# A two-layer diffusion trunk: modulation panels multiplied on VectorE, layer 0's last panels spread over three stages

## The chip, the core and the metric

The kernel runs on one core of a Trainium2 chip. The metric is the time of one execution on the device, in microseconds. It is given as the median of several runs; the profile is of one more execution.

## The reference

One step of a trunk with two layers over 640 tokens of width 1024: 128 prompt tokens and 512 latent tokens, in float32. In each layer a modulation vector of 6 x 1024 numbers is made from each of two conditions (one for the prompt, one for the latents), and then

```
mod = silu(cond) @ w_ada + b_ada
sh1, sc1, g1, sh2, sc2, g2 = split(mod, 6)
h = rmsnorm(x, norm_mix) * (1 + sc1) + sh1
x = x + g1 * mixer(h)
h = rmsnorm(x, norm_ffn) * (1 + sc2) + sh2
x = x + g2 * ((silu(h @ w_gate) * (h @ w_up)) @ w_down)
```

Layer 0's mixer is one input projection, then attention (8 heads of 64, the prompt over itself, the latents over the latents and 128 cached tokens) beside a state space scan in both directions (8 heads, chunks of 128 tokens, two groups of B and C), and one output projection. For each chunk the scan makes exp of differences of running sums of the decays, times C.B, times x, and adds C times the decayed state. Layer 1's mixer is retention with 4 heads. The FFN is 2816 wide.

## The kernel before, in words

Every engine has its instructions written out by hand, in one order per engine, with semaphores between them. The activations lie feature-major in SBUF; x is `xT`, the modulated h is split in a high and a low part (`h_hi`, `h_lo`), and so is every panel of weights: SyncE loads 1 MB (1024 x 256) into `raw0` or `raw1`, ScalarE writes `w_hi` (`split_hi`, L1086), VectorE `w_lo` (`split_lo`, L1448), and TensorE multiplies three products (`tile_a`, L579, 48 matmuls of 320 columns for 128 features; `tile_b`, L605, for 128 tokens in the input projection). VectorE subtracts a panel's low part only after ScalarE's high part, and that one is written when TensorE has left the slot's older panel.

**Modulation.** `w_ada` of a layer is 24 panels of 256 columns. `ada_job` (L638) multiplies one on TensorE: `scond`, the SiLU of both conditions in 2 of 32 columns, is the stationary operand, and eight fp32 matmuls of 256 columns go to four strips of partitions of one bank, `ROWS`. ScalarE copies the rows (`ada_rows`, L1091), and before the next panel `ada_turn` (L613) turns them to columns by two fp32 matmuls that also add the four strips. The columns collect in `ADA`. Layer 0's panels 0 to 7 are multiplied at the start (they give the first shift and scale). Its panels 8 to 23 are multiplied in the scan, from three buffers (`ada_raw0`, `raw0`, `raw1`), one or two per unit. Layer 1's panels 0 and 1 are multiplied in layer 0's output projection, 2 to 23 in layer 0's FFN, one behind each gate/up panel, from two buffers.

**The stages.** Times are those of the profile. Up to 63 us setup, first panels, norm. To 156 the input projection: three panels of q, k, v token by token (`tile_b`, five tiles each), then x, B, C, z. To 189 the convolution, the normed and rotated q and k, and dt, mostly on VectorE. To 286 the attention: 20 pairs, four of the prompt and 16 of the latents. In pair p TensorE makes the scores (`scores_of`, L739), VectorE the maximum, ScalarE the exponentials with their sum, GpSimd a diagonal of 1/sum; then TensorE turns the probabilities of pair p-1 (`turn_of`, L769) and multiplies pair p-2 by v (`att_of`, L758).

The scan runs from 286 to 375. TensorE makes running sums (L791), turned x and B, and C.B (L811). VectorE spreads the running sums per head (`by_head`, L1728) and makes xw (`weighted`, L1738); GpSimd makes xd, ten instructions (L2082), as soon as x is there. `ecum_of` (L830) and ScalarE give the decays on the states' partitions, `local_states` (L839) a chunk's own states into three banks, `step` (L1749, L1754) runs the states through the chunks. Then ten units of five chunks and two groups: `exponents` (L869 to L871, three matmuls for each direction: the sums per head, minus the sums along the tokens, the mask), ScalarE's exponential (L1285), VectorE's product with C.B (L1799, `m_ready`), and `outputs` (L893, L897). `exponents` of the next unit stand before a unit's panel and its `outputs`. VectorE also multiplies the decays by C (L1781) and reads y (`y_in`, L1787).

To 447 the output projection in two halves with the norm of y between them, `into_x` (L1542) and squares on VectorE. Then rms, `modulate` (L1508, L1520) and layer 0's FFN to 960: three chunks of 8, 8 and 6 gate/up panels, each chunk followed by four down panels. In an iteration ScalarE takes SiLU of the first tile, VectorE multiplies with the second (`gu32`, L1856), subtracts the low part of the next weight panel and of gu (L1865). Layer 1 follows, up to 2098; its panels are not touched.

SyncE's queue issues all loads in one order. A load waits for its buffer, and what is behind it in the queue waits too: `panel` for `w_lo` of the slot, `ada_panel` for the panel two before.

## Time and profile before

| | |
|---|---|
| median of 3 runs | 2093.09 us (2089.72 to 2094.92) |
| the profiled execution | 2099.29 us, its span 2097.7 us |
| granted TensorE clock, mean | 0.967 of full |
| busy, share of the span | TensorE 95%, VectorE 49%, ScalarE 27%, GpSimd 3% |
| the chain that ended last | TensorE 89%, VectorE 6%, ScalarE 2% |

Times in the profile are from the span's start. PE is TensorE's products, PEld its weight loads, DVE VectorE, ACT ScalarE, POOL GpSimd, SPq SyncE's queue. An fp32 matmul of 4 bytes without the r format shows as two records: an `ada_turn` has four, a panel's eight matmuls sixteen. Matmuls overlap, so the time of one is read from start to start.

### The profile page before, as it was taken

What the parts mean: (1) busy time and instruction counts of PE and PEld (TensorE: products, weight loads), DVE (VectorE), ACT (ScalarE), POOL (GpSimd) and SP (SyncE); (2) the same over time, 40 slices, a digit from 0 to 9 for tenths busy, and PEclk for the clock granted to TensorE, in tenths of its full rate; (3) what the DMA queues carried; (4) which work ended last, traced back from release to release, by engine and by line L of the source; (5) the groups of instructions that cost most, each with busy time, mean ns of one, the idle gap of its engine ahead of it and who ended that gap; (6) DMA issues with size and microseconds to landing.
All of it is one profiled execution on the core that took longest, in us unless ns stands there. A gap on an engine that the chain in (4) does not pass through costs nothing.

```text
span 2097.7 us, 32318 instructions
## 1 busy us (share of the span) xinstructions
PE 1989.3 (95%) x13455; PEld 1850.9 (88%) x13455; DVE 1032.8 (49%) x1472; ACT 563.3 (27%) x736; POOL 71.3 (3%) x118
## 2 busy tenths in 40 slices
PE   6999989889999999997999999999998999999997
PEld 3897856889999999997889889889888999999997
DVE  5377564782243234246646546645657235225335
ACT  2325432222212221223322332332333221221221
POOL 0001230000000000001010010010000000000000
PEclk7898988989999999999999999999998999999998
DMA  8320007344433433423212222122111222222211
GB/s 262 89 83 21 2 23 239 86 141 121 155 106 100 121 101 101 144 77 110 81 66 70 76 69 82 61 69 82 61 53 48 80 80 61 80 80 71 71 60 51
DMA packets 213535, 185.29 MB, mean 88 GB/s; under 512 B 10865, under 2 KB 198705, under 8 KB 213425
## 3 DMA queue, kind: packets, MB, share of 16 engines
q1 hardware_dynamic: 209504, 172.27, 26.7%
q0 software_dynamic: 3616, 11.29, 1.6%
q8 instruction: 89, 1.46, 0.3%
q14 instruction: 21, 0.17, 0.0%
q10 hardware_dynamic: 305, 0.10, 0.0%
HBM read 176.42 MB, written 7.21 MB: 88 GB/s over the span
## 4 chain that ended last, share of the span: by engine, by line
PE 89%; DVE 6%; ACT 2%; issue 1%; DMA 1%; SPq 0%; POOL 0%; ACTq 0%; DVEq 0%; POOLq 0%
PE acc L579 63%; PE acc L982 4%; PE mix L638 2%; PE acc L1013 2%; PE acc L1029 2%; PE acc L605 2%; PE acc L592 2%; PE acc L769 2%; PE mix L1002 1%; PE mix L982 1%; PE mix L739 1%; PE acc L758 1%; PE mix L613 1%; PE mix L653 1%; DVE h_lo L1520 1%
## 5 line engine op out<-in xcount | busy, mean ns | idle before, releaser
L579 PE MATMUL acc<-h_hi,w_hi 128*128 128x320 f32 x2144 | 495.6, 312 | 22.2 <-DVE h_lo L1520 6.3
L579 PE MATMUL acc<-h_lo,w_hi 128*128 128x320 f32 x2144 | 491.1, 310 | 4.3 <-issue 4.3
L579 PE MATMUL acc<-h_hi,w_lo 128*128 128x320 f32 x2144 | 490.2, 310 | 0.0
L579 PEld LDWEIGHTS acc<-h_hi,w_hi 128*128 128x128 f32 x2144 | 358.3, 189 | 37.3 <-issue 29.1
L1086 ACT ACTIVATE w_hi<-raw 128x2048 fp32r<-128x2048 f32 x112 | 214.3, 1914 | 653.0 <-PE acc L579 634.4
L579 PEld LDWEIGHTS acc<-h_hi,w_lo 128*128 128x128 f32 x2144 | 360.4, 189 | 4.7 <-issue 4.7
L579 PEld LDWEIGHTS acc<-h_lo,w_hi 128*128 128x128 f32 x2144 | 360.5, 189 | 0.0
L1448 DVE TENSOR_TENSOR w_lo<-raw,w_hi 128x2048 fp32r<-128x2048 f32 x112 | 256.7, 2292 | 199.4 <-ACT w_hi L1086 195.7
L1856 DVE TENSOR_TENSOR gu<-silu_g,acc 128x640 f32<-128x640 f32 x44 | 36.1, 821 | 416.8 <-PE acc L579 408.3
L1542 DVE SCALAR_TENSOR_TENSOR xT<-acc,mod,xT 128x128 f32<-128x128 f32 (+2 forms) x288 | 108.8, 433 | 140.6 <-PE acc L579 139.0
L579 PE MATMUL acc<-gu_hi,w_hi 128*128 128x320 f32 x704 | 160.7, 309 | 0.7 <-DVE gu_lo L1865 0.7
L579 PE MATMUL acc<-gu_hi,w_lo 128*128 128x320 f32 x704 | 160.4, 309 | 0.0
L579 PE MATMUL acc<-gu_lo,w_hi 128*128 128x320 f32 x704 | 160.2, 309 | 0.0
L579 PEld LDWEIGHTS acc<-gu_hi,w_hi 128*128 128x128 f32 x704 | 117.5, 188 | 2.2 <-issue 1.2
L579 PEld LDWEIGHTS acc<-gu_lo,w_hi 128*128 128x128 f32 x704 | 117.7, 188 | 0.0
L579 PEld LDWEIGHTS acc<-gu_hi,w_lo 128*128 128x128 f32 x704 | 117.6, 188 | 0.0
L1322 ACT ACTIVATE silu_g<-acc 128x640 f32<-128x640 f32 x44 | 31.1, 706 | 212.2 <-PE acc L579 205.9
L1470 DVE TENSOR_TENSOR sq_sum<-sq_sum,sq 128x640 f32<-128x640 f32 x99 | 81.7, 825 | 3.4
L1468 DVE TENSOR_TENSOR sq<-xT 128x640 f32<-128x640 f32 x84 | 69.4, 826 | 11.8 <-DVE xT L1542 6.6
L579 PE MATMUL acc<-yg_hi,w_hi 128*128 128x320 f32 x256 | 58.6, 311 | 3.3 <-DVE yg_lo L2015 3.3
L579 PE MATMUL acc<-yg_hi,w_lo 128*128 128x320 f32 x256 | 58.2, 309 | 0.0
L579 PE MATMUL acc<-yg_lo,w_hi 128*128 128x320 f32 x256 | 58.1, 309 | 0.0
(322 smaller groups left out, 2449.6 us busy)
## 6 DMA issues: line engine op xcount, KB each, us to landing
ada_raw<-in_l_w_ada_dram SPq DMA_DIRECT2D x64, 512.0 KB, 4.6
raw<-in_l_w_in_dram SPq DMA_DIRECT2D x64, 512.0 KB, 4.4
raw<-in_l_w_gate_dram SPq DMA_DIRECT2D x44, 512.0 KB, 4.0
raw<-in_l_w_up_dram SPq DMA_DIRECT2D x44, 512.0 KB, 5.3
raw<-in_l_w_down_dram SPq DMA_DIRECT2D x32, 512.0 KB, 4.5
raw<-in_l_w_out_dram SPq DMA_DIRECT2D x24, 512.0 KB, 4.5
raw<-in_l_w_ada_dram SPq DMA_DIRECT2D x22, 512.0 KB, 4.7
raw<-in_l_w_down_dram SPq DMA_DIRECT2D x16, 384.0 KB, 3.7
```

What stands on the lines that cost most here:

```text
L579: last = mm(acc[:, 2 * r + b, 0:HALF], w[:, k * cols + col:k * cols + col + P], x[:, k, b * HALF:(b + 1) * HALF], start=(k == 0 and n == 0 ...
L592: last = mm(acc[:, 2 * r[c] + b, 0:HALF], w[:, k * W + c * P:k * W + (c + 1) * P], x[:, k, b * HALF:(b + 1) * HALF], start=(k == 0 and n = ...
L605: last = mm(acc[:, 2 * r, 0:W], x[:, k, tok(t)], w[:, k * W:(k + 1) * W], start=(k == 0 and n == 0), stop=(k == KT - 1 and n == 2))
L638: last = mm(ROWS[32 * q:32 * q + 32, :], scond[:, k, :], w[:, k * W:(k + 1) * W], start=(turn == 0), stop=(turn == KT // 4 - 1))
L769: last = mm(acc[:, g, m * P:(m + 1) * P], probs[:, p % 2, g, m * P:(m + 1) * P], rdiag[:, (2 * p + g) % 4, :], start=True, stop=True)
L982: last = mm(V_BANKS[t], a[:, x, tok(t)], w[:, cols], start=(x == 0 and n == 0), stop=(x == KT - 1 and n == 2))
L1013: last = mm(acc[:, v, :], a, x, start=(b == 0 and k == 0 and m == 0), stop=(b == 1 and k == 1 and m == 2))
L1086: act(w_hi[s][:, :], raw[s][:, :], ACT.Copy).then_inc(S[f"w_hi{s}"], ac.up(f"w_hi{s}"))
L1448: ins = tt(w_lo[s][:, :], raw[s][:, :], w_hi[s][:, :].bitcast(f32), ALU.subtract)
L1468: tt(sq[:, :], src, src, ALU.mult).then_inc(S["dve"], v.up("dve"))
L1470: tt(sq_sum[:, :], sq_sum[:, :], sq[:, :], ALU.add).then_inc(S["dve"], v.up("dve"))
L1542: ins = st3(xT[:, d, dst], acc[:, 2 * r + b, src], mod[l][:, GA[m] + d, c:c + 1], xT[:, d, dst], ALU.mult, ALU.add)
```

## The change

- Layer 1's 24 panels are multiplied on VectorE in layer 0's FFN. `ada_products`: for each of 8 blocks of 128 rows and each condition, one instruction over 128 x 256 multiplies the panel's block by the condition's column (a scalar per partition) and adds it to `ada_sum` (in `tbuf`). `ada_add` on TensorE then sums over the partitions: four fp32 matmuls with `ada_sum` stationary and one column of ones, straight to `ADA`. One panel stands ahead of each gate/up iteration on VectorE, its add behind that iteration's tiles on TensorE; two panels stand in the first and the second down projection. The two jobs in the output projection, the row copies on ScalarE and SyncE's two loads ahead of the FFN are gone.
- Layer 0's panels 8 to 11 are multiplied in the same way in the input projection: products before the first, behind the first (one) and behind the second panel's low part (two), adds behind tiles (1,1), (1,4), (2,2), (2,4).
- Panels 12 to 14 stay TensorE jobs, in the attention's pairs 1 to 3 of the prompt. Panels 15 to 23 stay in the scan: three by the first exponents, then one per unit up to unit 6.
- The scan is reordered. An exponent is two matmuls: `L_all` and `R_all` hold on 128 partitions what the first two of three held on 64; ScalarE fills their constant halves during the attention and four scaled copies in the scan. Decays and exponents go through one ring of four banks. `local_states` uses one bank and waits for the step before. The prompt's units come between the steps. GpSimd's xd waits until four xw are made.

```diff
+            for n in ADA_DVE[0:2]:
+                ada_panel(w_ada, n * W)
...
+                if j == 3:
+                    for n in ADA_DVE[2:]:
+                        ada_panel(w_ada, n * W)
...
+            for n in ADA_PE:
+                k = ring_slot(n)
+                if n >= ADA_PE[3]:
...
+                else:
+                    eng.wait_ge(S["ada_used"], ADA_PE[0] - 1)
...
-            for n in range(2):
-                ada_panel(I["l1_w_ada"], n * W)
...
-                                ada_panel(I["l1_w_ada"], (i * 2 + s + f0 + 2) * W)
+                                ada_panel(I["l1_w_ada"], (i * 2 + s + f0 + m) * W)
...
+                        if l == 0 and m < 2 and j == 0:
+                            ada_panel(I["l1_w_ada"], (f0 + nf + m) * W)
...
+            def ada_add(l, n, b_):
+
+                eng.wait_ge(S["row_in"], pe.next("row_in"))
+                for b in range(2):
+                    for c in range(2):
+                        last = mm(ADA[:, l, bass.ds(n * 2 + b, 1), c:c + 1].rearrange("p o c -> p (o c)"),
+                                  ada_sum[b_][:, c, b * P:(b + 1) * P], ones[:, 0:1], start=True, stop=True)
+                last.then_inc(S["ada_turned"], pe.up("ada_turned"))
...
+            pe.skip("ada_in0", 32 * 2)
+            ADA_PLACES = [(1, 1), (1, 4), (2, 2), (2, 4)]
             for j in range(8):
...
                         tile_b(s, t, "h_ready" if j == 0 and t == 0 else None)
+                        if (j, t) in ADA_PLACES:
+                            n = ADA_DVE[0] + ADA_PLACES.index((j, t))
+                            ada_add(0, n, n % 2)
...
+            jobs = iter(ADA_PE)
+            ada_next = lambda: (lambda n: ada_job(0, n, n > ADA_PE[0]))(next(jobs))
             for p in range(NP + 2):
+                if p == 4:
+                    ada_turn(0, ADA_PE[2])
                 if p < NP:
                     scores_of(p)
+                if 1 <= p < 4:
+                    ada_next()
...
+            def ring(k):
+
+                kind, t, g = RING[k]
+                out = acc[:, k % 4, :]
+                if k >= 4:
+                    eng.wait_ge(S["arg_read"], k - 3)
+                if kind == "ecum":
+                    eng.wait_ge(S["r_ready"], R_ORDER.index(t) + 1)
+                    ins = mm(out, sel_wide[:, g, :], R_of(t), start=True, stop=True)
+                else:
+                    (t, g), d = chunks[t], g
+                    eng.wait_ge(S["r_ready"], R_ORDER.index(t) + 1)
+                    mm(out, L_all[:, 2 * d + g, tok(t)], R_of(t), start=True, stop=False)
+                    ins = mm(out, ident_r[:, :], mask_r[:, d, :].unsqueeze(1).broadcast_to([P, 4, P]), start=False, stop=True)
+                ins.then_inc(S["arg_made"], pe.up("arg_made"))
...
+                if s > 1:
+                    eng.wait_ge(S["z_ready"], s - 1)
...
-                    out, dg = acc[:, (2 * u + d) % 4, :], 2 * d + g
-                    mm(out, sel_dg[0:64, dg:dg + 1].broadcast_to([64, P]), R_of(t), start=True, stop=False)
-                    mm(out, cumx[:, tok(t)], sel_of[0:64, dg, :].unsqueeze(2).broadcast_to([64, 4, P]), start=False, stop=False)
-                    ins = mm(out, ident_r[:, :], mask_r[:, d, :].unsqueeze(1).broadcast_to([P, 4, P]), start=False, stop=True)
-                    ins.then_inc(S["arg_made"], pe.up("arg_made"))
...
-                        eng.wait_ge(S["s_out_ready"], 1)
+                        eng.wait_ge(S["g_read"], 4)
...
+            eng.wait_ge(S["xt_read"], TT)
+            c_dot_b(0, [acc[:, 2 + g, 0:P] for g in range(2)]).then_inc(S["g_made"], pe.up("g_made"))
+            eng.wait_ge(S["fill_ready"], 1)
+            ring(0)
+            ring(1)
+            ada_next()
+            eng.wait_ge(S["g_read"], 4)
+            ring(2)
+            ring(3)
+            eng.wait_ge(S["l_ready"], 1)
+            ring(4)
+            ring(5)
+            local_states(1)
+            for k in range(6, 10):
+                ring(k)
+            ada_next()
+            ring(10)
+            ring(11)
+            outputs(0)
+            local_states(2)
+            ada_next()
+            for k in range(12, 14):
+                ring(k)
+            outputs(1)
+            local_states(3)
+            local_states(4)
+            for u in range(2, 2 * TT):
                 if u + 1 < 2 * TT:
-                    exponents(u + 1)
-                ada_next()
+                    for d in range(2):
+                        ring(ring_at["expo", u + 1, d])
+                if u < 7:
+                    ada_next()
                 outputs(u)
-                if ADA_AFTER[u] > 1:
-                    ada_next()
             ada_turn(0, ADA_JOBS - 1)
...
-                if j == 0:
-                    eng.wait_ge(S["mod_read"], pe.next("mod_read"))
-                ada_job(1, j, j > 0)
...
                     if l == 0:
-                        ada_job(1, f + s_ + 2, slot=s_)
...
+                        ada_add(1, f + s_ + m, (s_ + m) % 2)
...
+                        if l == 0 and m < 2 and j == 1:
+                            ada_add(1, f0 + nf + m, m % 2)
...
+                if 1 <= p < 4:
+                    ada_rows()
...
+                if 6 <= p < 10:
+                    act(L_all[0:64, p - 6, :], sel_dg[0:64, p - 6:p - 5].broadcast_to([64, N]), ACT.Copy)
+                if 10 <= p < 15:
+                    ins = act(four(R_all[64:128, p - 10, :]), sel4[64:128, :].unsqueeze(2).broadcast_to([64, 4, P]), ACT.Copy)
+                    if p == 14:
+                        ins.then_inc(S["fill_ready"], ac.up("fill_ready"))
...
+            exponentials(0)
+            exponentials(1)
+            ada_rows()
+            eng.wait_ge(S["cumT_lo"], ac.next("cumT_lo"))
+            for dg in range(4):
+                ins = act(L_all[64:128, dg, :], cumx[64:128, :].bitcast(f32), ACT.Copy, scale=sel_dg[64:128, dg:dg + 1])
+            ins.then_inc(S["l_ready"], ac.up("l_ready"))
+            for k in range(2, 10):
+                exponentials(k)
+            ada_rows()
+            exponentials(10)
+            exponentials(11)
             ada_rows()
             for s in range(2):
...
+            eng.wait_ge(S["ce_ready"], 8)
...
+            ada_slot = [0]
+
+            def ada_products():
+
+                s = ada_slot[0] % 2
+                ada_slot[0] += 1
+                eng.wait_ge(S[f"ada_in{s}"], v.next(f"ada_in{s}", 32))
+                eng.wait_ge(S["ada_turned"], v.now("ada_turned", 1))
+                for k in range(KT):
+                    if k:
+                        eng.wait_ge(S[v.last], v.ended())
+                    for c in range(2):
+                        w = ada_raw[s][:, k * W:(k + 1) * W]
+                        if k == 0:
+                            ins = ts(ada_sum[s][:, c, :], w, scond[:, k, c:c + 1], None, ALU.mult)
+                        else:
+                            ins = st3(ada_sum[s][:, c, :], w, scond[:, k, c:c + 1], ada_sum[s][:, c, :], ALU.mult, ALU.add)
+                    ins.then_inc(S["dve"], v.up("dve"))
+                eng.wait_ge(S[v.last], v.ended())
+                eng.sem_inc(S["ada_used"], v.told("ada_used"))
+                eng.sem_inc(S["row_in"], v.told("row_in"))
+                v.skip("ada_turned")
...
+            ada_products()
...
+                for _ in range((1, 2, 0, 0, 0, 0, 0, 0)[j]):
+                    ada_products()
...
+            for t in R_ORDER[0:2]:
+                by_head(t)
             eng.wait_ge(S["wst_exp"], v.next("wst_exp"))
...
             weighted(1)
-            by_head(2)
-            by_head(3)
+            for t in R_ORDER[2:]:
+                by_head(t)
             weighted(2)
-            by_head(4)
             eng.wait_ge(S["s0_ready"], v.next("s0_ready"))
             step(1)
+            eng.wait_ge(S["g_read"], 4)
+            decayed_gram(0)
             weighted(3)
             weighted(4)
             step(2)
+            decayed_gram(1)
             step(3)
             eng.wait_ge(S["loc_made"], 4)
-            ins = eng.tensor_copy(s_out[:, :, :].rearrange("p h d -> p (h d)"), LOCAL[4])
...
-            eng.wait_ge(S["g_read"], 4)
             eng.wait_ge(S["c2_ready"], 1)
+            decayed_c(1, 0)
+            decayed_c(1, 1)
             for u, (t, g) in enumerate(chunks):
-                for d in range(2):
-                    eng.wait_ge(S["e_ready"], 2 * u + d + 1)
-                    ins = tt(e_of(u, d), e_of(u, d), G[:, g, t, :].unsqueeze(1).broadcast_to([P, 4, P]), ALU.mult)
-                    ins.then_inc(S["m_ready"], v.up("m_ready"))
+                if t == 0:
+                    continue
+                decayed_gram(u)
...
+                    if l == 0:
+                        per |= {"dve": 2 + 2 * KT, "ada_in0": 32, "ada_in1": 32, "ada_turned": 2, "row_in": 2, "ada_used": 2}
...
+                            if l == 0:
+                                ada_products()
...
+                        if l == 0 and m < 2 and j == 0:
+                            ada_products()
...
+            eng.wait_ge(S["xw_ready"], 4)
```

## Rows read from the trace of the kernel before

**Rows 1.** TensorE's timeline in layer 0's FFN: start us, us, engine, line, operation, out<-in, count.
```profile
506.36 0.50 PE L613 MATMUL mix<-fold,ada_row 128*128 128x2 f32 x4
506.79 1.07 PE L638 MATMUL mix<-ada_raw,scond 128*32 128x256 f32 x16
...
521.97 0.50 PE L613 MATMUL mix<-fold,ada_row 128*128 128x2 f32 x4
```

**Rows 2.** The chain that ended last, in order of time: layer 1's FFN.
```profile
1621.61 408.55 PE acc L579 x2784
```

**Rows 3.** Stretches of the scan: us, busy PE PEld DVE ACT POOL, clock, DMA share, GB/s.
```profile
286.00:325.00 39.00, 31.36 (x181) 17.61 (x183) 27.19 (x33) 12.65 (x26) 13.80 (x10) 0.71 0.17 55
325.00:379.00 54.00, 50.81 (x537) 33.13 (x534) 28.34 (x52) 18.82 (x38) 0.00 (x0) 0.97 0.84 254
```

**Rows 4.** The timeline of the scan's first half; in brackets idle time before, and its releaser.
```profile
292.68 1.29 DVE L1738 TENSOR_TENSOR xw<-x_tok,wdt 128x512 f32<-128x512 f32 x2
...
294.28 13.80 POOL L2082 TENSOR_TENSOR xd<-x_tok,dt_tok 128x512 f32<-128x512 f32 x10 [12.98 <-ACT x_tok L1251]
...
304.73 4.50 DVE L1738 TENSOR_TENSOR xw<-x_tok,wdt 128x512 f32<-128x512 f32 x4
307.32 1.98 PE L839 MATMUL mix<-xw,b_tok 128*64 128x256 f32 x8 [5.25 <-DVE xw L1738]
```

**Rows 5.** VectorE's groups by form: count, busy us, mean ns, idle before.
```profile
L1640 DVE SCALAR_TENSOR_TENSOR conv<-xpad,vec,conv 128x644 f32<-128x644 f32 x24 | 20.3, 886 | 0.4
...
L1520 DVE SCALAR_TENSOR_TENSOR h_lo<-tbuf,mod,h_hi 128x512 fp32r<-128x512 f32 x16 | 11.9, 746 | 0.0
...
L1520 DVE SCALAR_TENSOR_TENSOR h_lo<-tbuf,mod,h_hi 128x128 fp32r<-128x128 f32 x16 | 5.6, 347 | 1.1 <-ACT h_hi L1115 1.1
...
L1636 DVE TENSOR_SCALAR conv<-xpad,vec 128x644 f32<-128x644 f32 x6 | 3.0, 551 | 0.0
```

**Rows 6.** VectorE's timeline at the start of layer 0's FFN and inside it.
```profile
470.39 1.01 DVE L1520 SCALAR_TENSOR_TENSOR h_lo<-sq,mod,h_hi 128x128 fp32r<-128x128 f32 x2 [0.23 <-ACT h_hi L1115]
...
475.43 0.82 DVE L1856 TENSOR_TENSOR gu<-silu_g,acc 128x640 f32<-128x640 f32 x1 [4.02 <-PE acc L592]
...
526.33 0.82 DVE L1865 TENSOR_TENSOR gu_lo<-gu,gu_hi 128x640 f32 x1
```

**Rows 7.** ScalarE's timeline in the out projection.
```profile
432.66 1.92 ACT L1086 ACTIVATE w_hi<-raw 128x2048 fp32r<-128x2048 f32 x1 [12.66 <-DMA raw<-in_l_w_up_dram]
```

**Rows 8.** ScalarE's and VectorE's timeline in the input projection.
```profile
91.28 0.38 ACT L1158 ACTIVATE qkv<-acc 128x256 f32<-128x256 f32 x1 [2.50 <-PE acc L605]
...
93.73 2.29 DVE L1448 TENSOR_TENSOR w_lo<-raw,w_hi 128x2048 fp32r<-128x2048 f32 x1 [12.11 <-ACT w_hi L1086]
```

**Rows 9.** Busy time by stretch in the prompt's attention; one row of ScalarE's timeline in a later pair.
```profile
190.00:192.00 2.00, 0.57 (x5) 0.38 (x5) 0.76 (x5) 1.29 (x5) 0.74 (x2) 1.00 0.00 0
...
194.00:196.00 2.00, 2.00 (x10) 1.51 (x8) 0.52 (x3) 1.07 (x5) 1.82 (x7) 0.50 0.00 0
...
246.84 0.80 ACT L1227 ACTIVATE probs<-mix,nmax 128x640 f32<-128x640 f32 x1 [2.80 <-DVE nmax L1700]
```

**Rows 10.** TensorE's timeline in the scan's second half: third output, a unit, the last output.
```profile
336.09 0.66 PE L893 MATMUL mix<-tbuf,xd 128*64 128x128 f32 x8
...
345.58 0.49 PE L869 MATMUL acc<-R_lat,sel_dg 64*128 64x512 f32 x1
...
347.63 0.50 PE L613 MATMUL mix<-fold,ada_row 128*128 128x2 f32 x4
...
349.06 0.66 PE L893 MATMUL mix<-tbuf,xd 128*64 128x128 f32 x8
...
350.52 0.49 PE L869 MATMUL acc<-R_lat,sel_dg 64*128 64x512 f32 x1
...
374.80 0.39 PE L897 MATMUL mix<-ecum,ada_raw 128*64 128x128 f32 x4
```

**Rows 11.** Busy time by stretch just before the scan's clock rises.
```profile
324.00:326.00 2.00, 2.00 (x20) 1.33 (x14) 0.29 (x1) 1.19 (x3) 0.00 (x0) 0.50 0.07 11
```

More of the change, by code:

```diff
@@ L140 @@
     "vec_T vec_read cond no_cond": "small vectors turned, copied; SiLU of the conditions; the zeros beside them",
-    "ada_used row_in ada_turned mod_read gain_ready": "a panel multiplied, its rows copied, turned to columns; columns read; gains made",
+    "ada_used row_in ada_turned mod_read gain_ready": "a panel multiplied, its rows (layer 1: its sums by partition) in SBUF, turned to columns; columns read; gains made",
     "sq_done stat mean root": "squares added over tiles, over partitions (on TensorE), their mean, its root",
@@ L231, in trunk_kernel @@
         h32 = sb("h32", [P, N])
+        ada_sum = [tbuf[:, i, 0:2 * W].rearrange("p (c n) -> p c n", c=2) for i in range(2)]
         nbuf = (tbuf[:, 0, :], tbuf[:, 1, :], h32, sq)
@@ L1306, in _ @@
                 split_hi()
-                ada_rows()
             def ffn(l):
```

185 lines of the change are left out of this document (82 added, 103 removed).

## The prediction

> **What bounds the kernel now.** I read TensorE's timeline in a long part first, then the chain that ended last, then the table of stretches, then the timeline where TensorE waits. In layer 0's FFN TensorE never rests: a gate/up panel and its modulation job return every 15.61 us, from one row turn to the next (506.36 to 521.97), at the full clock [rows 1]. The same 96 products without a job cost 14.09 us in layer 1's FFN, where 2784 of them take 408.55 us [rows 2]. So one job with its turn costs 15.61 - 14.09 = 1.52 us of path, and every microsecond taken off TensorE there is a microsecond of time. Then the stretches: the scan's second half (325 to 379) is the same, 50.8 of 54 us busy at a granted clock of 0.97. Its first half (286 to 325) is different: 31.4 of 39 us at 0.71 [rows 3]. TensorE waits 5.25 us for VectorE's xw, and VectorE is slow there because GpSimd multiplies xd beside it: two xw took 1.29 us when GpSimd was just starting, four took 4.50 us inside its 13.80 us [rows 4]. The profiled execution took 2099.29 us, 6.2 above the median of the runs (2093.09); the terms are differences and are taken from either.
>
> **What a panel on VectorE costs.** Sixteen instructions over 128x256: two plain products, then fourteen with an addition, in pairs, a wait after each pair. The trace has no such row at 256. The same form took 347 ns over 128 and 746 over 512 [rows 5], so 480 by interpolation. In the convolution's pairs 24 of 886 ns were busy 20.3 us, so the next starts 40 ns before the last ends; a pair is then about 0.92 us, seven are 6.4, the plain pair 0.55 (551 ns over 644 for one): **6.95 us a panel**. Ends: 5.0 (all at 347 with overlap) and 9.0 (no overlap, more lost at the waits). The return of the sums is four matmuls per panel; a turn of two, the same fp32 form with one or two columns, takes 506.79 - 506.36 = 0.43 us [rows 1], so four take 0.86.
>
> **Layer 0's FFN: -9.7.** 22 panels give 1.52 - 0.86 = 0.66 us each, 14.5. The two panels placed in the down projections pay 0.86 each, 1.7, where nothing was before. VectorE ends its part of a panel 5.1 us after TensorE's last matmul (gu_lo ends at 527.15, the matmuls at 522.1) [rows 6]; the products end at 12.1, the new sums are wanted at 14.1. Cover is 2 us; if a panel takes over 8.9 us, the add waits, and with it every later tile. ScalarE loses its row copies, and SyncE waits for a buffer that VectorE frees at 12.1 instead of TensorE at 15, a whole iteration ahead of use. The uncovered place is the first iteration. VectorE ends layer 0's modulation at 471.4 and had 4.02 us free before the first gu at 475.43 [rows 6]. Now 6.95 us of products stand in that hole, so the sums come at 478.4 while TensorE arrives at 475.1: 3.3 us lost, once, perhaps 1.7 more if the clock falls there. -14.5 + 1.7 + 3.3 = -9.5, with -0.2 for the turn after the last panel. Ends -12 and -3.
>
> **The out projection: -1.5.** Two jobs of 1.52 leave it. One stood behind the last tile, beside VectorE's squares, and gives nothing. The other gives its 1.5 only if VectorE keeps up. It was held back by ScalarE's high part, which waited 12.66 us for the w_up panel [rows 7]; SyncE now issues that panel before the modulation panels. Ends 0 and -3.
>
> **The input projection: +6.1.** Four panels go on VectorE, four adds on TensorE, 3.4 us. Panel 8 is done long before its place (VectorE had 12 us free), panel 9 by about 88.6. Panel 10 is behind the low part of the second weight panel, which starts at 93.73 and ends at 96.0 [rows 8]; moved by one add to 96.85, the products end at 103.8. TensorE comes to its place behind tile 2 of the third panel, 8.6 us after the second panel's end (91.2 + 1.7), at 101.5: 2.4 us of waiting. Panel 11 ends at 110.8, its place is at 110.6 by then: 0.3. Sum 3.4 + 2.4 + 0.3 = 6.1, and the stage behind it starts later by all of it. Queued behind the waits: on TensorE tiles 3 and 4; on SyncE two weight panels behind the wait for panel 9's products, needed 15 us later. Ends +3.4 (5 us a panel) and +10 (9 us).
>
> **The prompt's attention: +2.5.** Three jobs and turns, 4.3 us at the full clock, 8.6 at half; the clock was 0.50 at 194 to 196, after TensorE was busy 0.57 of 2 us at 190 to 192 [rows 9]. The pairs are a chain over three engines (scores, maximum, exponentials, next scores); what it leaves idle on TensorE up to 206 I put at some 3 us, which the jobs fill. That leaves 1.3 to 5.6, or -2 if the denser work brings the clock back sooner. The row is nearest to the half clock, but for a part of the stretch only: I take 2.5. Nine fills of L_all and R_all, 0.6 to 0.7 us each (an estimate from the 0.6 us copies), go into ScalarE's 2.80 us of idleness per pair [rows 9]: nothing; over 2.8 they would delay the maximum's exponentials.
>
> **The scan: -10.** Nine jobs instead of sixteen; exponents by two matmuls instead of three; one ring of four banks; the states' steps in another order; xd held until two xw pairs are made. Second half first, because rows give it whole. Before: the third output starts at 336.1, the last ends at 375.1, 39.0 us. A unit with one job runs from 345.58 to 350.52: exponents 2.05, turn and job 1.43, output 1.46 [rows 10]. After: eight outputs 11.7, six pairs of exponents at 2 x 0.72 = 8.6 (two thirds of 1.03 each, and a little), four jobs 5.7: 26.0, and the last three units, without jobs, are paced by VectorE (some 3 to 4 us each with y and h_lo), which adds 3. 29 against 39: **-10**, if the third output starts at the same time. It hangs on a longer chain: ScalarE's four L copies (to about 302), first exponents and local states (305 to 306.5), step 1 beside GpSimd's xd (5.6 us, to 311), gram and output 0 (314), local states 2, step 2, gram, local 3, step 3, local 4, s_out, two decayed C, gram: four state steps and grams of VectorE at 2.8 and 1.4 and three matmul groups at 1 or 2 us. It ends at 330 with the full clock, 336 to 338 with the half. I take 336, since TensorE has holes of about 3 us in it. Ends -16 and 0.
>
> What the clock does decides between these. In 324 to 326 TensorE was busy the whole time, and had been since 307, at 0.50 of the clock, the lower level [rows 11]; full came behind 326. The Trainium skill (TensorE: Matmul & The Clock Gate, Part 1) says that sustained activity releases the throttle. By it the first half would run nearly full and the scan would give 16. The row speaks against it, and I keep 10.
>
> **Sum.** 6.1 + 2.5 - 10 - 1.5 - 9.7 = -12.6: 2086.7 against the profiled 2099.29, 2080.5 against the median.
>
> **Rivals.**
> A: the clock returns early in the scan, 6 us more: 2074.5. For it: both exponent matmuls now use all 128 rows, where two of three used 64. Against: 307 to 326. The skill's rule above would give this. 0.20.
> B: the chain in the scan's first half eats the second's gain, third output at 346: 2090.5. For it: one LOCAL bank puts three steps and three matmul groups in a row. Against: before, the same steps also stood in a row. 0.17.
> C, slower: the scan's units stay at half clock to the end, because each output now waits on VectorE. 26 us of TensorE become 52, the scan ends at 389 instead of 375, and the sum is +11.4: 2104.5. It decides if more than three units (4.3 us extra each) run at half. For it: jobs that filled the waits are gone. Against: the same loop ran at full behind 326. 0.08.
> D: a panel takes 10 us on VectorE. Each of 20 FFN iterations waits 1.2 us and the input projection pays 12: 2110. Against: [rows 5]. 0.07.
> That the change does less than it says I exclude: sixteen panels are 4 + 3 + 9 in its queues.
>
> **How the numbers follow.** Forecast 0.48, 2080.5, from about 2075 to 2086. A measurement of this kernel tells 0.3%, 6.3 us, from no change: faster is below 2086.8. The forecast and A lie there, with 0.03 of B: 0.71. The rest of B and little of C: 0.17. Slower 0.12. The range takes A with 4 us below, and B with 4 above: 2070 to 2094; C and D stay out.
>
> **What would show it.** FFN period near 14.95 us without w_ada matmuls; one wait of about 3 us at the first add; TensorE waiting for VectorE's sums once or twice at 101 to 111; the third output near 345 (336 moved by 8.6), units of 4.3 us, the clock there at 1.0. Wrong is: adds waiting in every FFN iteration, a clock of 0.5 in the units, or a third output later by over 5 us against its stage's start.

## The result and the profile after

The changed kernel takes 2075.63 us (median of 4 runs, 2074.14 to 2078.12) against 2092.95 for the kernel before (4 runs): 17.3 us less, a ratio of 0.9916 with a 95% interval of 0.9898 to 0.9933. The forecast was 2080.5, faster. The profiled execution took 2075.03, so its trace stands for the median. That of before (2099.29) does not quite: the kernel before comes out at two levels by itself, at one unchanged place in the scan, and its profile shows the upper one (first experiment). The stage table therefore has a second profile of before, at the lower level.

The page of the kernel after: the span, TensorE's busy time, the clock in 40 slices, the chain that ended last.

```profile
span 2073.5 us, 32367 instructions
...
PE 1957.8 (94%) x13099; PEld 1849.8 (89%) x13099; DVE 1217.5 (59%) x1924; ACT 563.9 (27%) x721; POOL 69.5 (3%) x120
...
PEclk8899999989999999998999999999998999999998
...
PE 87%; DVE 8%; ACT 2%; issue 2%; DMA 1%; SPq 1%; ACTq 0%; DVEq 0%
```

VectorE went from 49% to 59% of the span, TensorE lost 31.5 us of busy time (1989.3 before). By stage, from the first product of each in TensorE's timeline (us):

| stage | before | before, lower level | after | after - lower level | forecast |
|---|---|---|---|---|---|
| setup | 50.6 | 48.7 | 49.0 | +0.3 | 0 |
| input projection, convolution | 134.9 | 135.2 | 143.2 | +8.0 | +6.1 |
| attention | 101.1 | 100.5 | 101.1 | +0.6 | +2.5 |
| scan | 92.2 | 86.6 | 72.7 | -13.9 | -10 |
| out projection | 70.8 | 70.6 | 68.7 | -1.9 | -1.5 |
| norm | 9.7 | 9.7 | 8.8 | -0.9 | 0 |
| layer 0's FFN | 503.7 | 503.6 | 498.4 | -5.2 | -9.7 |
| norm | 8.8 | 8.8 | 9.8 | +1.0 | 0 |
| layer 1's mixer | 624.1 | 623.4 | 619.7 | -3.7 | 0 |
| span | 2097.7 | 2089.1 | 2073.5 | -15.6 | -12.6 |

Layer 1's norm and FFN, which the table leaves out, take 502 us in all three profiles. The sum came near because misses of both signs met in it. Now the rows, in the order of the steps.

**An FFN iteration.** TensorE's timeline (start, us, engine, line, operation), two adds of sums one iteration apart, the counterpart of [rows 1]:

```profile
496.35 0.95 PE L638 MATMUL mix<-squares,tbuf 128*128 128x1 f32 x8
497.16 0.55 PE L595 MATMUL acc<-h_hi,w_hi 128*128 128x320 f32 x2
...
511.32 0.95 PE L638 MATMUL mix<-squares,tbuf 128*128 128x1 f32 x8
```

The period is 511.32 - 496.35 = 14.97 us where it was 15.61, and the add occupies 497.16 - 496.35 = 0.81. VectorE's timeline inside that iteration, and the group by form from the list of groups (count | busy us, mean ns | idle before):

```profile
487.22 0.61 DVE L1620 TENSOR_SCALAR tbuf<-ada_raw,scond 128x256 f32<-128x256 f32 x2 [0.67 <-DVE gu_lo L1963]
487.87 6.38 DVE L1622 SCALAR_TENSOR_TENSOR tbuf<-ada_raw,scond,tbuf 128x256 f32<-128x256 f32 x14
```

```profile
L1622 DVE SCALAR_TENSOR_TENSOR tbuf<-ada_raw,scond,tbuf 128x256 f32<-128x256 f32 x392 | 172.7, 482 | 7.0
```

A panel takes 494.25 - 487.22 = 7.03 us and ends 2.1 us ahead of its add.

**The first iteration** is the exception. TensorE's timeline there, in brackets its idle time before and the releaser, then VectorE's, then the busy time of a stretch in it (columns as in [rows 3]):

```profile
463.25 1.87 PE L638 MATMUL mix<-squares,tbuf 128*128 128x1 f32 x8 [2.73 <-DVEq L1626]
464.98 0.88 PE L595 MATMUL acc<-h_hi,w_hi 128*128 128x320 f32 x2
```

```profile
456.00 0.62 DVE L1620 TENSOR_SCALAR tbuf<-ada_raw,scond 128x256 f32<-128x256 f32 x2 [0.34 <-DVE h_lo L1575]
456.66 6.38 DVE L1622 SCALAR_TENSOR_TENSOR tbuf<-ada_raw,scond,tbuf 128x256 f32<-128x256 f32 x14
463.45 0.82 DVE L1954 TENSOR_TENSOR gu<-silu_g,acc 128x640 f32<-128x640 f32 x1 [0.42 <-DVE tbuf L1622]
```

```profile
464.00:466.00 2.00, 2.00 (x10) 2.00 (x10) 1.66 (x2) 0.74 (x1) 0.00 (x0) 0.50 0.77 218
```

TensorE waits 2.73 us, and the clock is at its lower level behind it: the add takes 1.73 instead of 0.81.

**The input projection.** TensorE's only wait for sums, and the stretches behind it:

```profile
101.67 1.87 PE L638 MATMUL mix<-squares,tbuf 128*128 128x1 f32 x8 [2.42 <-DVEq L1626]
```

```profile
102.00:104.00 2.00, 2.00 (x11) 2.00 (x11) 1.93 (x6) 0.00 (x0) 0.00 (x0) 0.50 0.00 0
...
106.00:108.00 2.00, 2.00 (x11) 2.00 (x11) 1.89 (x6) 0.00 (x0) 0.00 (x0) 0.50 0.00 0
108.00:110.00 2.00, 2.00 (x19) 2.00 (x18) 0.81 (x2) 0.38 (x1) 0.00 (x0) 0.97 0.03 8
```

The 2.42 us wait costs more than itself: until 108, 11 matmuls start in 2 us where 19 do after it.

**Attention.** The stretches that answer to [rows 9]; there the clock was 0.50 from 193.4 on:

```profile
198.00:200.00 2.00, 1.91 (x24) 1.21 (x24) 0.65 (x3) 1.10 (x6) 1.17 (x2) 1.00 0.00 0
...
212.00:214.00 2.00, 2.00 (x12) 1.16 (x9) 1.05 (x2) 0.13 (x1) 0.00 (x0) 0.52 0.00 0
214.00:216.00 2.00, 2.00 (x20) 1.99 (x18) 0.74 (x2) 2.00 (x6) 0.00 (x0) 1.00 0.00 0
```

With the jobs between the pairs TensorE is busy for 1.9 to 2.0 of every 2 us from 198 to 208, and the clock stays full until 210.5; half clock lasts from there to 213.9, 3.4 us, where before it was 13.6 (193.4 to 207.1).

**The scan** in two stretches, the counterpart of [rows 3]; then the two places where its clock falls, and TensorE's third output, one unit with its job and the last output, the counterpart of [rows 10]:

```profile
293.00:335.00 42.00, 31.02 (x253) 20.86 (x253) 26.12 (x40) 17.73 (x35) 10.95 (x10) 0.90 0.32 101
335.00:366.00 31.00, 25.57 (x304) 19.72 (x300) 23.96 (x45) 15.07 (x25) 0.00 (x0) 0.97 0.52 136
...
309.00:313.00 4.00, 4.00 (x15) 2.20 (x15) 1.64 (x2) 2.28 (x6) 4.00 (x5) 0.57 0.19 62
...
331.00:333.00 2.00, 2.00 (x7) 1.62 (x7) 1.97 (x4) 0.00 (x0) 0.00 (x0) 0.50 0.00 0
```

```profile
335.26 1.12 PE L902 MATMUL mix<-tbuf,xd 128*64 128x128 f32 x8
...
349.23 0.50 PE L867 MATMUL acc<-R_all,L_all 128*128 128x512 f32 x1
349.56 0.39 PE L868 MATMUL acc<-mask_r,ident_r 128*128 128x512 f32 x1
349.79 0.39 PE L867 MATMUL acc<-R_all,L_all 128*128 128x512 f32 x1
...
350.25 0.50 PE L629 MATMUL mix<-fold,ada_row 128*128 128x2 f32 x4
...
351.69 0.66 PE L902 MATMUL mix<-tbuf,xd 128*64 128x128 f32 x8
...
353.15 0.50 PE L867 MATMUL acc<-R_all,L_all 128*128 128x512 f32 x1
...
362.47 0.39 PE L906 MATMUL mix<-ecum,ada_raw 128*64 128x128 f32 x4
```

The granted clock of the first half is 0.90 where it was 0.71; it is at the lower level from 309.5 to 312.9 and from 330.0 to 336.8. A unit with a job takes 353.15 - 349.23 = 3.92 us (4.94 before), its exponents 350.25 - 349.23 = 1.02 (2.05). From the third output to the last one's end it is 27.6 us where it was 39.0. Its start is 42.0 us behind the stage's (335.26 - 293.29), where before it was 49.6 at the upper level and 44.0 at the lower.

**The out projection.** ScalarE's high part of the w_up panel, in [rows 7] behind a wait of 12.66 us:

```profile
431.42 1.91 ACT L1118 ACTIVATE w_hi<-raw 128x2048 fp32r<-128x2048 f32 x1 [12.16 <-PE acc L595]
```

A transfer ended that wait before; now it is TensorE's leaving the older panel, 0.5 us sooner. The stage is 1.9 us shorter.

**Layer 1's mixer,** which no line of the change touches, is 3.7 us shorter. That is no term of the forecast, and the second group of experiments is about it.

### The profile page after: what moved, and what is told of

Same layout as the page of the kernel before. It is cut to its first block, busy times and chain, and to the rows that moved or that the text cites. A ratio compares the mean times of both kernels' runs of the same rounds, so it can differ in the third digit from the quotient of the medians.

```text
span 2073.5 us, 32367 instructions
## 1 busy us (share of the span) xinstructions
PE 1957.8 (94%) x13099; PEld 1849.8 (89%) x13099; DVE 1217.5 (59%) x1924; ACT 563.9 (27%) x721; POOL 69.5 (3%) x120
## 3 DMA queue, kind: packets, MB, share of 16 engines
q8 instruction: 88, 1.44, 0.3%
## 4 chain that ended last, share of the span: by engine, by line
PE 87%; DVE 8%; ACT 2%; issue 2%; DMA 1%; SPq 1%; ACTq 0%; DVEq 0%
PE acc L595 63%; PE acc L1014 4%; PE acc L1045 2%; PE acc L1061 2%; PE acc L621 2%; PE acc L795 2%; PE mix L1034 1%; PE mix L638 1%; PE mix L765 1%; PE mix L1014 1%; PE acc L784 1%; DVE h_lo L1575 1%; PE mix L659 1%; PE mix L674 1%; PE acc L608 1%
## 5 line engine op out<-in xcount | busy, mean ns | idle before, releaser
L1622 DVE SCALAR_TENSOR_TENSOR tbuf<-ada_raw,scond,tbuf 128x256 f32<-128x256 f32 x392 | 172.7, 482 | 7.0
```

What stands on the lines that cost most here:

```text
L1622: ins = st3(ada_sum[s][:, c, :], w, scond[:, k, c:c + 1], ada_sum[s][:, c, :], ALU.mult, ALU.add)
```

## The experiments

They ran on several chips, so ratios are to the kernel before in runs beside each on the same chip. Its own median there was 2090.86, 2097.21, 2093.68 or 2096.61 us, so ratios of different groups compare only to some 0.3%. What an edit does is read from the stages.

### The kernel before, unchanged, two more times

Theory: the half clock in the scan's first half is one of two outcomes at one place. Rival: it belongs to the kernel, and the gain in the scan is all the change's. The first of the two runs also asks whether stops in layer 1's mixer repeat (next group).

> The kernel before, unchanged, for a second profile. Its first profile took 2099.29 us, 6.2 above the median, and in layer 1's mixer, which the change does not touch, TensorE stood six times (8.0 us in all) with nothing to wait for, against three times (4.0 us) in the kernel after. Theory P (the places of the instructions set these stops): six again, 8.0 us, and from layer 1's start to the end the same time within 1 us. Rival E (they belong to one execution): another number of stops, and the profiled time nearer the median, 2092 to 2095.

> The kernel before once more, for its two levels of time (2090 and 2098 in the runs beside these experiments, both profiles at the upper one). Theory C (the two levels are the moment at which the clock comes back in the scan: at 312 or at 326): if the profiled execution takes 2089 to 2092, its scan takes 85 us and the clock is full from about 312; if it takes 2096 to 2100, its scan takes 92 us and the clock is full from 326. Rival: a time at one level with the other level's scan.

Measured: 2098.19 and 2090.67 us. Setup and input projection together differ by 2.2 us (186.1 and 183.9 at their end), the scan by 5.5 (92.1 and 86.6), every other stage by at most 0.3. The six stops in layer 1's mixer came again in both, 7.4 us in all. Busy time by stretch in the scan of the second of them:

```profile
308.00:312.00 4.00, 4.00 (x28) 2.04 (x28) 3.86 (x7) 0.70 (x3) 0.00 (x0) 0.54 0.07 15
312.00:316.00 4.00, 4.00 (x14) 1.77 (x12) 2.98 (x5) 1.19 (x2) 0.00 (x0) 1.00 0.74 251
```

and its timeline where TensorE waits for xw:

```profile
305.12 1.98 PE L839 MATMUL mix<-xw,b_tok 128*64 128x256 f32 x8 [5.26 <-DVE xw L1738]
```

The wait is the same 5.26 us (5.25 in [rows 4]), yet behind it the clock is back to full at 312, after 7 us of work, where before [rows 11] it took 19 (307 to 326). So 5.5 us of the scan are one kernel's two outcomes, and the profiles' difference of 24.2 us is 15.6 against the lower level. The median's 17.3 lies between the two. Which level is the more frequent differs: of the 19 runs of before beside the first set of experiments, 13 took 2089.8 to 2092.3 and 6 took 2095.3 to 2099.95; of 25 beside the second set, on another chip, 5 took 2089.8 to 2092.1 and 20 took 2095.05 to 2101.6. What decides between them was not found.

The new scan has not shown the late return. In the seven profiles of kernels that have it, half clock lasts at most 6.9 us at a stretch and the scan takes 71.2 to 73.1 us. Of the seven with the old scan, five have half clock for 24 us (92.1 to 92.2 us of scan) and two for 10 (86.6 and 85.3). So the scan gains 13.9 us on a kernel before at its lower level and 19.5 on one at its upper level.

### The FFN's part alone, and the place of layer 1's loop

ffn_only is the kernel before with the change's FFN: VectorE's products and TensorE's adds in it, the out projection's two jobs gone, the scan and all ahead of it as before.

```
-                        ada_job(1, f + s_ + 2, slot=s_)
+                        ada_add(1, f + s_ + m, (s_ + m) % 2)
...
-                ada_job(1, j, j > 0)
```

> The kernel before with only the part on layer 1's panels: VectorE's products, TensorE's adds, the two jobs of the out projection gone. Theory A (the parts add up): the input projection, attention and scan as before; out projection and norm 3.0 us less, the FFN 5.2 less (a period of 14.97 against 15.61, and some 7 us lost once behind the first iteration), so about 8 less in all: 2085. Rival B (the loss behind the first iteration is due to what the scan left behind): the FFN 10 us less, 13 in all, 2080. Rival C (the gain is all in the scan): within 3 us of 2093.

Measured: a ratio of 1.0027 (1.0012 to 1.0042), 0.3% more, where theory A had 8 us less. Part of it is the two levels: its profile has the late return in the scan, and six of its ten runs took 2098.9 to 2101.9 us, four 2093.0 to 2095.2. The FFN gained what it gained in the whole change, 498.3 us against 503.7, but layer 1's mixer, which isn't touched, took 633.3 instead of 624.1. The waits of TensorE from 900 to 1640 us, grouped (waited for: us in total, times, longest), show only one group that moved. First before, then after, then ffn_only:

```profile
PE acc L579 <- issue: 8.0, 6, 1.6
```

```profile
PE acc L595 <- issue: 4.0, 3, 1.7
```

```profile
PE acc L580 <- issue: 12.5, 3, 4.2
```

These are stops in which TensorE waits for nothing the profile shows, at the returns of the loop over layer 1's four heads. Three returns cost 8.0, 4.0 or 12.5 us. In ffn_only each of the three is followed by half clock. The first, in its timeline and its stretches:

```profile
1123.75 0.87 PE L580 MATMUL acc<-h_hi,w_hi 128*128 128x320 f32 x2 [4.16 <-issue]
```

```profile
1124.00:1128.00 4.00, 4.00 (x16) 4.00 (x17) 1.82 (x1) 0.00 (x0) 0.00 (x0) 0.50 0.23 46
```

The loop has 1754 of TensorE's instructions, counted in the built program. Theory: the price hangs on where the loop's code begins in TensorE's program, which any edit ahead of it shifts. Rival: it hangs on what the FFN left behind (VectorE's, SyncE's state). The test is a shift alone: waits that are already met, put ahead of TensorE's first transpose, move all that follows and change no work. Two waits make one instruction's place.

```
+            for _ in range(234):
+                eng.wait_ge(S["squares_in"], 16)
```

with 234 in the kernel after (117 places, which puts its loop at the place it has in ffn_only), 120 in ffn_only, 320 in the kernel before.

> The kernel after with 234 waits that are already met ahead of TensorE's first transpose, which stand in front of a wait for the small vectors' DMA; they move all of TensorE's later instructions by 117 places, so that layer 1's loop over the heads stands where it stood in the kernel with the FFN part alone. Theory P (the place of that loop decides how long TensorE stands at each return to its start): three stops of 4.2 us instead of 1.1 to 1.7, the clock falls behind them, layer 1's mixer takes 629 to 633 us instead of 619.7, the time is 9 to 13 us more, 2085 to 2089. Rival W (the stops come from what the kernel does, or from one execution): stops of 1.1 to 1.7 again, the time within 2 us of 2075.6.

> The FFN part alone, moved by 60 places in the same way, so that the loop over the heads stands early in its piece of the instructions. Theory P: three stops of 1.0 to 1.7 us, the mixer near 619.7, the time 2099 - 13 = 2086, about 5 under the kernel before; the FFN part is then worth its 6 us of layer 0. Rival W: stops of 4.2 us again and 2099.

> The kernel before, moved by 160 places, so that its loop over the heads stands where it stands in the kernel after. Theory P: three stops (4 us) instead of six (8 us), the mixer 619.7 instead of 623.5, the time 3 to 5 us under the kernel before. Then the change itself is worth about 4 us less than was measured. Rival W: six stops, the same time within 1 us.

Measured: ratios of 0.9979 (0.9963 to 0.9995), 0.995 (0.9934 to 0.9965) and 1.0019 (0.9999 to 1.0039). The pads cost 5.8, 1.5 and 7.9 us ahead of the first product, so the mixer's own time is what tells; the totals missed what was expected of them (after_pad took 17.7 us more than the kernel after, 9 to 13 expected; before_pad 3.9 more than before, 3 to 5 less expected). The same waits rows, in the same order:

```profile
PE acc L595 <- issue: 13.2, 3, 4.6
```

```profile
PE acc L580 <- issue: 4.3, 3, 1.5
```

```profile
PE acc L579 <- issue: 3.4, 3, 1.2
```

| kernel | loop's first instruction, mod 256 | stops, us (number) | layer 1's mixer, us |
|---|---|---|---|
| ffn_only_pad | 19 | 4.3 (3) | 619.8 |
| after | 98 | 4.0 (3) | 619.7 |
| before_pad | 98 | 3.4 (3) | 618.9 |
| before | 194 | 8.0 (6) | 624.1 |
| ffn_only | 215 | 12.5 (3) | 633.3 |
| after_pad | 215 | 13.2 (3) | 633.9 |

The rival fell: the mixer of one program with the same work moves by 14 us with its place (after against after_pad), and two different programs at one place agree (215: 633.3 and 633.9; 98: 619.7 and 618.9). The Trainium skill (Runtime: NRT & Kernel Launch, Instruction fetch mechanics) says that instructions are fetched in blocks of 256 and that a taken branch out of the blocks held stalls for a fetch. A dependence on the place modulo 256 agrees with that; four such places were seen, and why 215 is the worst stays open. The same section of the Trainium skill gives TensorE's store as 2048 instructions; this loop of 1754 would fit, and stops at every return all the same. The FFN's shorter loops return without a stop of over 0.15 us in the traces of before and after. So some 4 us of the change's 15.6 are not its work, and a reader of ffn_only's total alone would have taken a gain of 5.3 us in the FFN for a loss.

### xd held until xw is made

The change also holds GpSimd's xd back. before_hold adds that line to the kernel before; after_nohold takes it from the kernel after.

```
+            eng.wait_ge(S["xw_ready"], 4)
             for t in range(TT):
                 eng.wait_ge(S["xt_read"], X_ORDER.index(t) + 1)
```

> The kernel before with one wait more: GpSimd's xd starts only when four xw are made. Theory H (GpSimd beside VectorE is what makes the first half of the scan slow, by xw and by the clock that falls behind TensorE's wait of 5.25 us): two xw in 1.3 us, the wait for xw under 2 us, the granted clock full to at least 315, the third output 5 to 8 us ahead of 336.1, and the time 5 to 8 less, about 2086. Rival O (the order of the states' steps and the exponents sets the third output, not xd): the third output within 2 us of 336, time within 2 us of 2093.

> The kernel after without the wait of GpSimd's xd for four xw. Theory H: VectorE's first xw and the running sums per head are slowed beside GpSimd, the first local states come 3 us later or more, TensorE's clock falls there, the third output (335.3 now) 5 to 8 us later, time 5 to 8 more, about 2082. Rival O: the third output within 2 us, time within 2 us of 2075.6.

Measured: 0.999 (0.9977 to 1.0003) and 0.9913 (0.9896 to 0.9929; after itself 0.9916). In before_hold the wait shortens and the clock comes back at 312, in the profile as at the lower level:

```profile
305.53 1.97 PE L839 MATMUL mix<-xw,b_tok 128*64 128x256 f32 x8 [3.84 <-DVE xw L1738]
```

All its 10 runs lie between 2089.2 and 2092.1, none at the upper level. The wait is 1.4 us shorter, not under 2 us as theory H had it, and the median, 2090.28, is only 0.6 below the 2090.86 of before beside it, not 5 to 8. Without the hold, the new order of the states' steps has a slower xw pair (VectorE's timeline of after_nohold, then of the kernel after):

```profile
302.75 2.97 DVE L1821 TENSOR_TENSOR xw<-x_tok,wdt 128x512 f32<-128x512 f32 x2
```

```profile
302.75 1.28 DVE L1821 TENSOR_TENSOR xw<-x_tok,wdt 128x512 f32<-128x512 f32 x2
```

2.97 us instead of 1.28, with GpSimd multiplying beside it; but TensorE waits until 308.25 either way, for ScalarE's four copies to L_all, and the scan takes 72.5 us without the hold, 72.7 with it. So the hold is not what shortened the scan. Whether it is what kept before_hold at the lower level stays open: with 13 runs of before in 19 there, ten of ten come by chance about twice in 100 (an estimate from these counts).

### The input projection's last two adds later

```
-            ADA_PLACES = [(1, 1), (1, 4), (2, 2), (2, 4)]
+            ADA_PLACES = [(1, 1), (1, 4), (2, 4), (3, 0)]
```

> The kernel after with TensorE's adds of layer 0's panels 10 and 11 at later places: behind tile 4 of the third panel and behind the first tile of the fourth, instead of tiles 2 and 4 of the third. Theory L (the 9 us that the input projection got longer are 3.3 of adds, 2.4 of waiting and 3.1 of half clock behind the wait): no wait, the clock full from 80 to 115, the stage 5 to 6 us shorter (137.5 from the first product to the attention's first transpose instead of 143.2), the time 5 to 6 less, 2070. Rival V (VectorE is late anyway and the stage behind waits for the normed q and k): the stage at most 2.4 shorter, and no more than 2 us in the time.

Measured: 2071.19 us, 0.9881 (0.9854 to 0.9909); this interval overlaps that of the kernel after, so the stage is what tells. It takes 138.8 us instead of 143.2. No wait for sums is left in it, and the clock stays at full where it had fallen:

```profile
102.00:104.00 2.00, 2.00 (x19) 2.00 (x18) 1.65 (x5) 0.38 (x1) 0.00 (x0) 1.00 0.00 0
```

Of the 4.4 us gained 2.4 are the wait; the other 2.0 are most of the 2.9 that the half clock cost behind it (0.9 on the add, 2.0 on 22 matmuls that start every 0.21 us instead of 0.12). The four adds themselves, 3.2 us, remain.

### No panel in the FFN's first iteration

free_first multiplies panel n after the products of iteration n and adds it one iteration later, so VectorE's hole ahead of the first gu stays free; the last panels go to the three down projections, one each. best joins it with late_adds and takes the hold out. best2 moves the third of those panels away from the end: two in the first down, one in the second, none in the third; it has late_adds and keeps the hold. The adds as best2 has them:

```
-                    if l == 0:
-                        ada_add(1, f + s_ + m, (s_ + m) % 2)
+                    if l == 0 and not first:
+                        n = s_ + (m or -1)
+                        ada_add(1, f + n, n % 2)
...
-                        if l == 0 and m < 2 and j == 1:
-                            ada_add(1, f0 + nf + m, m % 2)
+                        if l == 0 and j in ((1, 3), (1,), ())[m]:
+                            n = nf + (j // 2 - 1 if m == 0 else m)
+                            ada_add(1, f0 + n, n % 2)
```

> The kernel after with no panel ahead of the FFN's first iteration: panel n stands ahead of iteration n + 1, one panel in each of the three down projections, 24 products and 24 adds as before. Theory F (the first iteration's panel stands in a hole of VectorE that is too short for it, and the wait also drops the clock): the wait of 2.7 us at the first add gone, the clock full from 450 on, the FFN 6 us shorter (492.4 from its first product to the norm behind it instead of 498.4), the time 2069.6. Rival M (the wait only moves, to the second iteration or to the third down projection, whose sums VectorE then makes beside its into_x): the FFN at most 2 us shorter.

> The three edits on top of the kernel after: late adds in the input projection, no panel ahead of the FFN's first iteration, xd not held. If the parts add up (4.4 to 4.9, 6 and 0 to 3), 2062 to 2065; if they share the same clock drops, 2066 to 2069.

> The kernel after with the late adds of the input projection, no panel ahead of the FFN's first iteration, and the two panels that are left in the first down projection (ahead of VectorE's first and third step there) instead of one each in all three; xd held as in the kernel after. Theory T (without the last panel in the third down projection, where TensorE's steps are 10.6 us and VectorE's 7 us of products push the next low part back by 3 to 4 us, the first iteration's gain stays): no wait of TensorE inside the FFN at all, 491 to 492.5 from its first product to the norm behind it, 6 less than the kernel with the late adds alone, 2065. Rival U (the third step of the first down projection is as full as the third down projection): the FFN near 495, 2068 to 2070.

Measured: free_first 2075.04 us, 0.9902 (0.9875 to 0.993), no gain on the kernel after; its FFN 495.6 us instead of 498.4. The first iteration's wait is gone, but its profile shows the panel in the third down standing ahead of VectorE's additions into x (VectorE's timeline):

```profile
894.64 0.62 DVE L1625 TENSOR_SCALAR tbuf<-ada_raw,scond 128x256 f32<-128x256 f32 x2 [0.28 <-DVE gu_lo L1967]
895.29 6.38 DVE L1627 SCALAR_TENSOR_TENSOR tbuf<-ada_raw,scond,tbuf 128x256 f32<-128x256 f32 x14
901.93 1.13 DVE L1602 SCALAR_TENSOR_TENSOR xT<-acc,mod,xT 128x128 f32<-128x128 f32 x3 [0.26 <-DVE tbuf L1627]
```

and TensorE then waits for the banks that those additions free:

```profile
903.27 0.87 PE L600 MATMUL acc<-gu_hi,w_hi 128*128 128x320 f32 x2 [2.43 <-DVEq L1605]
```

So one such stall was exchanged for another, as rival M had it. best took 2069.88, 0.9879 (0.9859 to 0.99), above both sums expected of it; it has that panel too. best2, without that panel, has no wait of TensorE inside the FFN; the stretch at its start (the counterpart of the one at 464 in the kernel after):

```profile
460.00:474.00 14.00, 14.00 (x99) 14.00 (x98) 10.38 (x20) 4.53 (x4) 0.00 (x0) 1.00 0.33 103
```

Its FFN takes 492.5 us, its input projection 138.6, and the total is 2066.57 us (2063.28 to 2067.29), 0.9857 (0.983 to 0.9884): faster than both kernels. The FFN has 5.9 us more gain than in the kernel after (498.4 - 492.5), near the 7.0 that the first iteration cost; 1.0 of that, the half clock at the stage's start, is in best2 too.

## Why the prediction was right, and where its sum was not

The forecast, faster by 12.6 us, was right and its size 5 us short. That it came so near is in part luck. The measured 2075.63 us is nearer to rival A's 2074.5 than to the forecast's 2080.5; the terms missed by up to 4.5 us, both ways; and the trace that they were read from shows the kernel before at its upper level, against which the scan alone gave 19.5 us, not 10. By its steps:

- **A panel on VectorE, 6.95 us:** 7.03; the form at 256, interpolated at 480 ns, measured 482. **The add, 0.86:** 0.81. **The period, 14.95:** 14.97. The cover of 2 us does hide the panel in every later iteration: rival D is out.
- **The FFN's first iteration, 3.3 us:** the step that failed. The wait was 2.73, near its size, but "perhaps 1.7 more if the clock falls there" was left out of the sum, and it fell: the add took 0.9 longer, nine pairs of matmuls behind it (464.98 to 469.92) took 4.94 us where a pair at full clock takes 0.293, 2.3 more; and some 1.0 was lost before the wait, where the stage's start was at half clock from 443.5 to 449.5 (before: 459.3 to 463.1). Sum 7.0, and 14.1 for 22 periods less 1.6 for two adds less 7.0 gives 5.5; the table has 5.2. best2 shows the same from the other side.
- **The input projection, 6.1:** +8.0. The wait came as worked out, 2.4, and the second one, 0.3, did not come. What was missed is again the clock behind the wait, 2.9. late_adds took wait and clock away and gave back 4.4.
- **The attention, 2.5:** +0.6. The step took half clock for part of the stretch; with the jobs there the clock instead stayed at full to 210.5. In the seven profiles with these jobs the attention has 3.4 to 6.8 us of half clock, in the seven without 10.3 to 13.7. That it is the jobs which keep the clock up is argued from these rows; no run moves them alone. The remark that denser work might bring the clock back was kept as an end of the range, and the 0.6 lies on its side.
- **The scan's second half, 29 us:** 27.6. Six exponent groups by two matmuls for each direction cost 1.02 each where 1.44 was put ("two thirds of 1.03 each, and a little"), 2.5 us in six. The last three units' waits, 0.76, 1.86 and 0.21, sum to 2.8; 3 was taken. The first output, still at half clock, gave some of it back (the first half of it 1.34 us, where in the unit shown it is 0.70). The shares of the scan's parts are read from rows; no run has the two-matmul exponents, the fewer jobs or the new order alone.
- **The scan's first half, 0:** the third output comes 2.0 us earlier than in the kernel before at its lower level, 7.6 earlier than in the profile of before. Rival A ("the clock returns early in the scan, 6 us more") named the mechanism: the granted clock was 0.90 there, and half only from 309.5 to 312.9 and from 330.0 to 336.8. Part of this is not the change's doing, for the kernel before has the early return too, in 13 of 19 runs on one chip and in 5 of 25 on another. The forecast's price of zero rested on [rows 11], a row of the upper level, and set the Trainium skill's rule aside for it. That rule (TensorE: Matmul & The Clock Gate, Part 1: sustained activity releases the throttle) came nearer here than the row, but the rows agree with it in direction only: with the same wait ahead, full clock came after 7 us of work in one profile and 19 in the other, and after 6.4 behind the input projection's wait (101.67 to 108.02). The states' new order left three waits of 2.8 to 3.0 us in the chain, as the forecast had it ("holes of about 3 us").
- **The out projection, 1.5:** -1.9. The stage takes 67.0 to 69.9 us in the seven profiles of kernels with the new scan, so an agreement to 0.4 us tests little.
- **Rivals B and C** did not come: the third output is not late against its stage's start, and the units run at full clock from 337 on.
- **Not in the forecast:** layer 1's mixer, -3.7, by the place of its loop, as the shifts showed (the kernel before, shifted to the same place, has 618.9). Without it the change gives about 12, close to the 12.6 forecast, but by sums that compensate: FFN and input projection 6.4 worse, scan and attention 5.8 better.

The norms' -0.9 and +1.0 go with the clock. Over the first norm's first 1.5 us it is 0.50 before (from 449.51), over its first 1.3 us 0.92 after (from 434.73); at the second norm's start it is 0.96 before (962.91 to 965) and 0.50 after (941 to 943). So the 1.0 lost at the FFN's start is what the norm ahead of it gained.

## What to carry to other kernels

A wait put on TensorE can cost itself and the half clock behind it: here 2.4 and 2.7 us of waiting cost 5.3 and 6.0 in all. Not every wait does: behind those of 1.42 and 2.76 us in the scan (to 317.04 and 324.43) the clock stayed full until 330. So work moved to an idle engine belongs where its result is wanted with time to spare, as the panels with 2.1 us of it in the FFN and those of late_adds, not just in time. Give the moved work a place in the receiver's own queue, too: the panel that was free in 21 iterations stalled TensorE in the first, where VectorE stood on the path. And before an edit is credited or blamed, look at the stages that it doesn't touch: a loop's place in the program moved one stage here by 14 us, nearly as much as the whole change.

## What the runs showed of the hardware that was not expected

- The loop of 1754 TensorE instructions stops at each return: 1.0 to 1.7 us a time at two places (mod 256), in two stops at a third (7.1 to 8.0 us for three returns), 4.1 to 4.6 us at a fourth. The place is set by everything ahead of it.
- The return of the clock after an equal wait differs between runs of one unchanged kernel: 7 us of work or 19, worth 5.5 us of the scan.
- A matmul of 128 rows and 512 columns that follows one of the same rows starts 0.23 us after it (349.56 to 349.79 in the unit shown); in the kernel before, between matmuls of 64 rows, the next start was 0.43 us behind the same mask matmul (346.22 to 346.65). Two of three replaced by one of 128 rows therefore saved half of the time, not a third.
- VectorE's xw pair takes 1.28 us alone and 2.97 beside GpSimd's products of the same tiles.
